# Three Fox units projected before the norm's factor, and the attention output's squares ahead of its weight splits

## The reference, cut to what matters

```python
# first block, layer 1
hn = rms_norm(h, ln_mix[i, 0])
m = diff_attention_mixer(hn, ...)             # ends in o @ w_o
h = h + rms_norm(m, ln_mix[i, 1])
f = swiglu(rms_norm(h, ln_ffn2[i, 0]), ffn2_w_gu[i], ffn2_w_down[i])
...
# second block, each layer l
mod = silu(c) @ ada_w[l] + ada_b[l]
shift, scale, gate = split(mod, 3)
h = rms_norm_2(x, norm_g[l]) * (1.0 + scale[:, None, :]) + shift[:, None, :]
y = even_mixer(h, ...) if l % 2 == 0 else odd_mixer(h, ...)
x = x + gate[:, None, :] * y
...
def odd_mixer(h, w_in, b_f, qnorm_g, knorm_g, w_out):
    proj = (h @ w_in).astype(jnp.float32)
    q, k, v, g, fl = jnp.split(proj, [...])
    ...
    o = o * jax.nn.silu(g)
    return o.astype(h.dtype) @ w_out
```

## Time and profile before

| | |
|---|---|
| median of 3 runs | 1335.21 us (1334.97 to 1335.21) |
| the profiled execution | 1334.41 us, span of its instructions 1332.6 us |
| TensorE busy | 98% of the span |
| VectorE, ScalarE, GpSimd busy | 69%, 61%, 10% |
| DMA | 237.70 MB read, 179 GB/s over the span |
| granted TensorE clock | 1.00 |

### The profile page before, as it was taken

How to read it: one execution, slowest core, us unless ns; L and a number is a source line. 1 busy time by engine, 2 the same in 40 slices (tenths; PEclk the granted TensorE clock), 3 DMA queues, 4 the chain that set the end, 5 groups by cost and what they waited for, 6 DMA issues and landing times.

```text
span 1332.6 us, 28059 instructions
## 1 busy us (share of the span) xinstructions
PE 1312.1 (98%) x10516; PEld 1281.2 (96%) x10516; DVE 924.2 (69%) x1506; ACT 809.0 (61%) x1576; POOL 127.3 (10%) x119
## 2 busy tenths in 40 slices
PE   8999999999999999999999999899999999999998
PEld 8999999999999999999999888899999899999898
DVE  7877556976777555877645877688875576576775
ACT  6766555446766565766654665777765453466773
POOL 2000012013000022000021211120002200010000
PEclk9999999999999999999999999999999999999999
DMA  6777554554677473677563543357756353445441
GB/s 242 236 222 224 193 220 156 184 168 155 219 233 219 158 263 110 222 231 217 165 252 111 168 144 100 127 188 239 238 192 254 122 159 95 127 156 185 136 129 62
DMA packets 64580, 240.54 MB, mean 181 GB/s; under 512 B 7840, under 2 KB 9360, under 8 KB 64496
## 3 DMA queue, kind: packets, MB, share of 16 engines
q1 hardware_dynamic: 63408, 238.84, 54.9%
q0 software_dynamic: 1088, 0.53, 0.2%
HBM read 237.70 MB, written 1.05 MB: 179 GB/s over the span
## 4 chain that ended last, share of the span: by engine, by line
PE 89%; DVE 5%; ACT 4%; issue 1%; DMA 1%; SPq 0%; ACTq 0%; DVEq 0%
PE bank L1917 26%; PE bank L1919 26%; PE bank L1918 26%; DVE w_lo L1168 2%; PE bank L1961 1%; PE bank L1968 1%; PE bank L1969 1%; PE bank L2301 1%; DVE h L1230 1%; ACT w_hi L643 1%; DVE arena L1224 1%; PE bank L2285 1%; PE bank L2284 1%; PE bank L2286 1%; ACT ln_t L674 0%
## 5 line engine op out<-in xcount | busy, mean ns | idle before, releaser
L1168 DVE TENSOR_TENSOR w_lo<-raw,w_hi 128x1024 fp32r<-128x1024 f32 (+2 forms) x376 | 493.2, 1317 | 221.6 <-ACT w_hi L643 221.5
L1917 PE MATMUL bank<-x_hl,w_hi 128*128 128x272 f32 (+1 forms) x2008 | 579.3, 288 | 2.1 <-DVE w_lo L1168 1.3
L1919 PE MATMUL bank<-x_hl,w_lo 128*128 128x272 f32 (+1 forms) x2008 | 574.7, 286 | 0.0
L1918 PE MATMUL bank<-x_hl,w_hi 128*128 128x272 f32 (+1 forms) x2008 | 572.3, 285 | 0.0
L643 ACT ACTIVATE w_hi<-raw 128x1024 fp32r<-128x1024 f32 (+2 forms) x376 | 410.2, 1097 | 175.2 <-PE bank L1919 99.9
L1917 PEld LDWEIGHTS bank<-x_hl,w_hi 128*128 128x128 f32 x2008 | 378.0, 188 | 3.2 <-DVE w_lo L1168 1.5
L1918 PEld LDWEIGHTS bank<-x_hl,w_hi 128*128 128x128 f32 x2008 | 380.5, 190 | 0.4
L1919 PEld LDWEIGHTS bank<-x_hl,w_lo 128*128 128x128 f32 x2008 | 377.4, 188 | 0.0
L1917 PE MATMUL bank<-a_hi,w_hi 128*128 128x272 f32 (+1 forms) x960 | 275.8, 287 | 0.9 <-DVE w_lo L1168 0.6
L1919 PE MATMUL bank<-a_hi,w_lo 128*128 128x272 f32 (+1 forms) x960 | 273.5, 285 | 0.0
L1918 PE MATMUL bank<-a_lo,w_hi 128*128 128x272 f32 (+1 forms) x960 | 273.0, 284 | 0.0
(11 more groups left out here) (286 smaller groups left out, 1256.4 us busy)
## 6 DMA issues: line engine op xcount, KB each, us to landing
raw<-w SPq DMA_DIRECT2D x312, 512.0 KB, 4.3
raw<-w SPq DMA_DIRECT2D x64, 704.0 KB, 5.8
ada_raw<-ada_w SPq DMA_DIRECT2D x48, 512.0 KB, 3.6
h<-x_in SPq DMA_DIRECT2D x2, 544.0 KB, 5.3
work<-bands SPq DMA_DIRECT2D x1, 544.0 KB, 6.7
out<-h SPq DMA_DIRECT2D x1, 512.0 KB, 2.9
out<-h SPq DMA_DIRECT2D x4, 128.0 KB, 2.3
arena<-arena POOLq DMA_DIRECT2D x28, 17.0 KB, 3.3
```

Source lines behind the costliest of these rows:

```text
L1168: ve.tensor_tensor(w_lo[:, s, cols], raw[:, s, cols], w_hi[:, s, cols].bitcast(F32), ALU.subtract).then_inc(w_lo_ready, 1)
L1917: te.matmul(dst, w_hi[:, s, a:a + P], rhs_hi, start=first, stop=False)
L1918: te.matmul(dst, w_hi[:, s, a:a + P], rhs_lo, start=False, stop=False)
L1919: return te.matmul(dst, w_lo[:, s, a:a + P], rhs_hi, start=False, stop=last)
```

## The change

Three things are changed.

1. **Fox entry.** Units 0, 1 and 2 are projected from `h` times `gs` alone, without the norm's factor `r` and without the shift. ScalarE makes the uppers (`raw_upper`, L1104 of the new file), VectorE the lowers (`bl`, L1280), and the matmuls get 264 columns: the 8 further ones hold the shift, copied there once (`sh` on ScalarE, L1101, and `sl` on VectorE, L1795). When a unit is done, VectorE multiplies its 256 columns by `r` (L1803) and copies the shift's product aside (L1804); this replaces ScalarE's copy of these three units, and SiLU gets it as a bias (three activations of 256 columns, L1223, and one of 1280, L1225, in place of one of 2048). Unit 3 and all later ones still need the normed input, which is now written over the raw one chunk by chunk, when TensorE has left the chunk. The sum over partitions moves between the chunks, GpSimd adds one more chunk, and the nine idle matmuls go.
2. **Attention output.** ScalarE does the first three narrow splits before the squares, the squares 4 to 7 ahead of the next stage's splits, and leaves the copies of 4, 5 and 6 to VectorE (a `tensor_scalar` each). TensorE does the first six chunks of unit 6 first, and all three sums behind unit 7.
3. **Loads.** In the four down-projection stages the load of a conditioning block moves: in quads 1 and 2 from between slots 1 and 2 to behind slot 3.

```diff
@@ scalar engine, attention output @@
-            out1("aout", "resa")
+            for s in range(3):
+                split_next("aout", 0, s)
+            for o in range(SLOTS):
+                aout_square(o)
+                aout_copy(o)
+                if o == 1:
+                    split_next("aout", 0, 3)
+            aout_square(4)
+            aout_square(5)
+            split_next("aout", 1, 0)
+            aout_square(6)
+            split_next("aout", 1, 1)
+            aout_square(7)
+            aout_copy(7)
+            split_next("aout", 1, 2)
+            res_norm("resa")
@@ scalar engine, Fox entry @@
             out2("eout", 0)
+            shift = mod[:, 1, 0, :].unsqueeze(2).broadcast_to([P, DC, COL])
+            sc.activation(x_hi[:, :, SEQ:SEQ + COL], shift, ACT.Copy).then_inc(act.step("preo", "sh"), 1)
...
+            sc.wait_ge(vec.sem, vec.at("preo0", "gs"))
             for c in range(DC):
                 if 4 <= c < 7:
                     split_next("eout", 1, c - 4)
+                if c == 5:
+                    raw_upper(2)
+                if c == 6:
+                    raw_upper(3)
                 pre_square("preo", c, (vec.sem, vec.at("eout", f"h{c % 4}", c // 4)))
-            pre_rms("preo")
+                if c == 2:
+                    raw_upper(0)
+                    raw_upper(1)
+                if c == 6:
+                    raw_upper(4)
+                    raw_upper(5)
+            raw_upper(6)
+            raw_upper(7)
+            rsqrt("preo", STAT[:, 0:SEQ], r_t[:, 0:SEQ], 1.0 / D, eps6, (pe.sem, pe.at("preo", "ss")))
+            split_next("eout", 1, 3)
             for c in range(DC):
+                if c < DC - 1:
+                    sc.wait_ge(pe.sem, pe.at("preo", f"a{c}"))
+                else:
+                    sc.wait_ge(unit_done, SLOTS * FIRST_QUAD["oin"] + BEHIND)
                 pre_upper("preo", c)
@@ vector engine, attention output @@
-            evac_out1("aout")
+            for s in range(SLOTS):
+                split_next("aout", 0, s)
+            for o in (4, 5, 6):
+                if o == 6:
+                    split_next("aout", 1, 0)
+                ve.wait_ge(act.sem, act.at("aout", f"sq{o}"))
+                ve.tensor_scalar(f[:, o, 0:SEQ], out1_bank("aout", 1, o - SLOTS)[:, 0:SEQ], gain("resa", o), None, ALU.mult
+                                 ).then_inc(vec.step("aout", f"f{o}"), 1)
+            split_next("aout", 1, 1)
+            split_next("aout", 1, 2)
@@ vector engine, Fox entry @@
+            ve.scalar_tensor_tensor(gs[:, 1, :], mod[:, 1, 1, :], 1.0, par("norm_g", 8, 8), ALU.add, ALU.mult
+                                    ).then_inc(vec.step("preo0", "gs"), 1)
+            ve.wait_ge(act.sem, act.at("preo", "sh"))
+            ve.tensor_tensor(x_lo[:, :, SEQ:SEQ + COL], mod[:, 1, 0, :].unsqueeze(2).broadcast_to([P, DC, COL]),
+                             x_hi[:, :, SEQ:SEQ + COL].bitcast(F32), ALU.subtract).then_inc(vec.step("preo0", "sl"), 1)
             out2("eout", 0)
             pre("preo")
...
+                ve.wait_ge(unit_done, SLOTS * FIRST_QUAD["oin"] + u + 1)
+                ve.tensor_tensor(fox_unit(u), fox_bank(u)[:, 0:SEQ], r_t[:, 0:SEQ], ALU.mult).then_inc(vec.step("behind", f"m{u}"), 1)
+                ve.tensor_copy(gate_bias[:, u:u + 1], fox_bank(u)[:, SEQ:SEQ + 1]).then_inc(vec.step("behind", f"w{u}"), 1)
...
             for u in range(GATES):
                 fox_split_lo(u)
+                if u < BEHIND:
+                    fox_behind(u)
@@ tensor engine, Fox entry (in place of first_quad) @@
+                for k in range(DC):
+                    te.wait_ge(act.sem, act.at("preo", f"b{k}"))
+                    for u in range(BEHIND):
+                        te.matmul(fox_bank(u)[:, 0:n], w_hi[:, u, k * P:(k + 1) * P], x_hi[:, k, 0:n], start=k == 0, stop=False)
+                        te.matmul(fox_bank(u)[:, 0:n], w_lo[:, u, k * P:(k + 1) * P], x_hi[:, k, 0:n], start=False, stop=False)
+                    if k:
+                        lower(k - 1)
+                    if k == 1:
+                        te.wait_ge(pool.sem, pool.at("preo", "add6"))
+                        te.matmul(STAT[:, 0:SEQ], ones[:, :], sq8[:, 0, 0:SEQ], start=True, stop=False)
+                        te.wait_ge(act.sem, act.at("preo", "sq7"))
+                        te.matmul(STAT[:, 0:SEQ], ones[:, :], sq8[:, DC - 1, 0:SEQ], start=False, stop=True).then_inc(pe.step("preo", "ss"), 1)
+                lower(DC - 1)
+                te.wait_ge(w_lo_ready, SLOTS * q + 4)
+                for k in range(DC):
+                    te.wait_ge(vec.sem, vec.at("preo", f"lo{k}"))
+                    last = product(bank[3][:, 0:SEQ], 3, k, x_hi[:, k, 0:SEQ], x_lo[:, k, 0:SEQ], k == 0, k == DC - 1)
```

More of the change, by code:

```diff
@@ L467, in build @@
         vec.phase("fl0", ["wlo0", "wlo1", "ib", "cb", "ob", "o64"])
+        vec.phase("behind", [a + str(u) for u in range(BEHIND) for a in ("m", "w")])
         for u in range(GATES):
-            act.phase(f"c{u}", ["c"])
+            if u >= BEHIND:
+                act.phase(f"c{u}", ["c"])
             if u == 3:
@@ L604, in _ @@
                 if stage[:2] == "dn":
-                    for i in range(3):
-                        load(stage, i, lambda: load_ada(k, 9 + i))
+                    load(stage, 0, lambda: load_ada(k, 9))
+                    for i in range(2):
+                        load(stage, 1 + i)
+                        load_ada(k, 10 + i)
+                    load(stage, 3)
                 else:
@@ L2409, in _ @@
                 last.then_inc(unit_done, 1)
-            te.wait_ge(pool.sem, pool.at("preo", "add5"))
-            te.matmul(STAT[:, 0:SEQ], ones[:, :], sq8[:, 0, 0:SEQ], start=True, stop=False).then_inc(pe.step("preo", "ss5"), 1)
-            pre("preo", range(6, DC))
-            keep_clock(9, bank[2])
             def fox_project(u):
```

106 lines of the change are left out of this document (78 added, 28 removed).

## The result

The changed kernel takes 1337.47 us (median of 20 runs, 1336.02 to 1338.84), the kernel before 1335.18 us (20 runs, 1334.20 to 1336.75). The medians lie 2.3 us apart; the ratio of the runs is 1.0015, 95% interval 1.0010 to 1.0021, so the changed kernel is slower by 2.0 us (1.3 to 2.8); 1336.5 was forecast. The profiled execution took 1336.19 us, with a span of 1334.4 and a granted clock of 1.0.

The account below looks back on a forecast made before the run. TensorE, busy for 98% of the span, was taken as the bound. Attention output -1.4, Fox +2.7 and loads 0 summed to +1.3 us: 1335.7 for the profiled execution, 1336.5 for the median, range 1332.9 to 1339.0.

Parts of the forecast that it names:

- attention output, first product by the factor: Attention output: VectorE's first product by the factor starts at 858.2 in place of 859.56, a gain of 1.4 us.
- start of the fifth unit: Output projection before Fox: TensorE wants the first lower part at 1169.42, gets it about 1171.3, a new 1.9 us stop.
- third Fox lower part, start of Fox: Fox entry: VectorE's third lower part ends at 1181.9, so TensorE starts Fox there, 1.1 us earlier than 1183.02.
- unit 3 done: Fox: unit 3, waiting for the normed chunks, ends at 1195.5 in place of 1194.93, +0.6 us.
- unit 6: Fox: waits for the bank freed by unit 4's late copy, starting at 1204.9 instead of 1202.4, +2.5 us.
- SiLU in pieces: Fox gates on ScalarE: four pieces take 2.1 us in place of 1.92, costing +0.2, between 0 and 0.4.
- Fox in all: All Fox-side changes together cost +2.7 us, with bounds 0 and +3.5.
- loads: Down projections: the new order of loads costs 0, since TensorE has no wait there.
- A: Fox side costs nothing, later slack swallows the late logarithm, only -1.4 is left: 1333.8 us; chance 0.20.
- B: Fox entry: lower parts not held, unit 4's copy in time, Fox starts 3.9 us earlier: 1332.2 us; chance 0.12.
- C: Attention output: GpSimd's adds are blocked and become its bound, +0.5 there, 1338.4 us in all; chance 0.12.
- D: TensorE falls to its lower clock behind two stops of about 2 us, +2 each: 1340.5 us; chance 0.08.

Follow-up runs that it names:

- experiment 4: Changed kernel with VectorE's lower part of the shift moved from ahead of the output projection's list to behind it: 1334.16 us, ratio 0.9994 to the kernel before.
- experiment 5: Changed kernel with ScalarE's copy of unit 4 put first, ahead of its wait for the forget gate's logarithm: 1335.80 us, ratio 1.0005 to the kernel before.
- experiment 6: Changed kernel with both the shift's lower part behind VectorE's list and unit 4's copy ahead of the logarithm wait: 1332.60 us, ratio 0.9981 to the kernel before.
- Experiment 7: Version with both mends, plus one SiLU instruction in place of four, VectorE adding the shift's column to three units: 1331.81 us, ratio 0.9975 to the kernel before.
- experiment 8: Version with both mends and one SiLU, plus twelve upper-part products ahead of TensorE's wait for the third lower part: ratio 0.9976 to the kernel before.
- Fox alone: Kernel before with all Fox-entry hunks of the change and no others: 1338.52 us, ratio 1.0029 to the kernel before.

## Why the prediction was right

1336.5 was forecast and 1337.47 measured, inside the range, and the change of +0.15% is within the 0.2% to which the prediction gave 0.62. By steps, on the clock before:

| step | forecast | in the trace |
|---|---|---|
| attention output, first product by the factor | 858.2, -1.4 | 858.28, -1.28; by B -1.49 |
| start of the fifth unit, late by | 1.9 | 1.90 (1171.32 against 1169.42), of it 1.73 in brackets |
| third Fox lower part, start of Fox | 1181.9 | 1181.9 (1180.81 + 1.12) |
| the factor | 1186.1 | 1185.8 (1184.30 + 0.42 + 1.12) |
| unit 3 done | 1195.5 | 1195.4 (1194.33 + 1.12) |
| logarithm's input | 1203.6 | 1203.4 (1201.82 + 0.41 + 1.12) |
| unit 6 | 1204.9, +2.5 | 1204.75, +2.27 (against 1202.48; forecast from 1202.4) |
| SiLU in pieces | +0.2 | +0.57 (starts 0.92 apart in place of 0.35) |
| Fox in all | +2.7 | +2.89 |
| loads | 0 | 0 |

The first two stops and the order of the chain come from laying the engines' lists beside each other and asking, at each wait, what stands behind it. Experiments 4 and 5 show that the two waits named are the causes: the shift's lower part ahead of VectorE's list costs 2.5 us, the copy of unit 4 behind the logarithm 1.5. Their sum is more than the 2.89 that Fox lost, because the change itself is worth about 1 us there once both are gone (experiment 6).

The term that was mis-sized is the SiLU. I took 0.31 for a piece of 256 columns, which is about the distance at which ScalarE's plain copies and squares of that width are followed by the next instruction; the three pieces lie 0.41 apart (1220.74 to 1221.96), and the one of 1280 takes 1.26 in place of 1.2. So the four take 2.48 and not 2.1, and the upper bound of 0.4 was passed as well. Experiment 7 confirms it: with one SiLU of 1.92 the stop of 0.64 is gone, and 0.57 us with it up to that matmul. That Fox's total came out so near, +2.7 for +2.89, is in part luck: unit 6 was 0.23 too dear in the forecast, the SiLU 0.37 too cheap.

The reason for the stop at unit 6 was given as one sum, +2.5, in which the late lower parts and the copy's place in the list were not told apart. They are two: with the late lower parts mended unit 6 still waits 1.25 us (experiment 4), and with the copy moved it doesn't wait, though the logarithm's input is as late as ever (experiment 5: it ends at 1202.45, 1202.20 on the clock of the changed kernel, against 1202.23). That "the first three units' early start is used up, because the chain of the norm still stands before unit 3" holds as well: experiment 8 starts Fox 1.46 us earlier and ends 0.36 earlier.

**The rivals.** A (Fox costs nothing) and B (neither stop is real) fell: the stops are in the trace, and Fox alone is slower by 1.8 to 4.1 parts in a thousand. C (GpSimd blocked) fell: one add of six at 1.44, where three were needed. The rule of the Trainium skill, SBUF — State Buffer, "Who interferes with whom", fits that one add, which was issued 0.38 us into a subtraction, and little else in the changed kernel's rows could show it: VectorE's other work beside the adds, the copies of units 4 and 5, reads a bank. For subtractions issued second the rows show no block: in the kernel before three of 256 elements start 0.56 us into an add of 0.72 to 0.73 and take 0.45 to 0.46 us, where two with no add beside them take 0.43 in the changed kernel.

D (TensorE at its lower clock behind stops of 2 us) was wrong in size, and may have been right in kind. In the profiled execution the granted clock is 1.00, the upper of the two levels, and the matmuls behind the stop at 1180.81 follow at 0.12, as elsewhere. But of the changed kernel's 20 runs only seven record 1.000; their median is 1336.19. The other 13 record 0.997 to 0.999, and their median is 1337.95, so 1.8 us more. A clock below 1.000 is on record for 20 of 37 runs of the three kernels that have both stops of 1.7 to 1.9 us (changed, Fox alone, copy first), for 3 of 11 with the shift behind, and for 10 of 105 of all others, the kernel before among them (7 of 56). Where in those runs the clock fell, and that it fell behind these stops, is not shown: every trace here is of an execution at 1.00. Nor does the recorded mean size the loss: one run with the shift behind has 0.949 at 1334.7 us.

This also bears on how near the forecast came. The prediction took the median to lie 0.8 us above the profiled execution, as before the change; now it lies 1.3 above. For the profiled execution 1335.7 was forecast and 1336.19 measured. At the full clock the change costs 1.2 us by the medians and 1.4 by the stretches, where +1.3 was forecast; most of the rest, up to the ratio's 2.0 (1.3 to 2.8), goes with the runs at a lower clock.
